# The first norm of a Hyena / mLSTM step, moved from token rows to feature rows

## The chip, the cores and the metric

The kernel runs on one core of one Trainium2 chip. The metric is the device time of one execution in microseconds, the median of three runs. Five engines matter. PE multiplies matrices (PEld is its weight load), DVE, ACT and POOL work element by element, and SP issues most of the DMA transfers. They meet only through semaphores.

## The reference

One layer of a diffusion backbone over 1024 latent tokens and 128 prompt tokens, each of 1024 features. What the change touches is the first norm and what it feeds:

```python
def _rmsnorm(x, w):
    xf = x.astype(F32)
    y = xf * lax.rsqrt(jnp.mean(xf * xf, axis=-1, keepdims=True) + EPS)
    return (y * w.astype(F32)).astype(x.dtype)
...
    h = _rmsnorm(x, p['norm_mix_w']) * (1 + scale_m) + shift_m
    proj = h @ p['w_in']
```

The mean of squares is over the features of one token; gain and shift differ for latent and prompt tokens. Beside it the reference makes the spectrum of a filter `k` from a small network, long before the projection needs it. Convolution, mLSTM, output projection, second norm and feed forward follow and are not touched.

## The kernel before, in words

Tokens come in nine tiles of 128, features in eight chunks of 128 (`KD`). Every large product is fp32 in three passes: each operand is split into a rounded part `hi` and a remainder `lo`, and `product` (lines 231, 233, 235) adds hi·hi, hi·lo and lo·hi in PSUM. A split costs one ACT instruction (hi) and one on DVE or POOL (lo).

**Stage A, the filter's spectra** (`filter_and_spectra`, one block of all engines). Twelve steps `spectrum(g)`, g = 0 to 11, of 24 matmuls of 256 columns each, write two PSUM banks each, in a ring of four pairs, `pair(g)`. For each step ACT copies one bank (L2072) and DVE combines it with the other (L2187 and L2188, or L2191); that signals `read`. After three steps a quarter of the spectrum is finished by `butterflies`, four instructions (L1628 to L1631): the first three quarters on POOL, the last one on DVE at the end of the block. SP stores each quarter to DRAM. Beside them the first norm runs by token row: x, nine tiles of 128 tokens by 1024 features, stays in SBUF; ACT takes the squares with their sum (L316), one tile in each step, DVE makes the means (L322), ACT the roots (L327), DVE the reciprocals (L332), ACT scales x in place (L337, nine instructions). SP loads x after the last modulation weights. POOL also splits two weight units (L180).

**Stage B, the projection** (`project_and_hyena`, the next block; a block starts when all engines have left the one before). x must stand by feature for the projection, so PE turns each chunk of it by transposes (`norm_chunk`, L1018): 24 chunks, eight for each group of tokens (`GROUPS`: tiles 0 to 2, 3 to 6, 7 and 8; in columns `PIECES`). DVE reads each turned chunk from PSUM with gain and shift (L1372), ACT makes hi (L1198), POOL two of three lo and DVE the third (L637). PE works on the projection's first two blocks of 128 outputs (items 0 and 1) piece by piece, as chunks come: piece 0 for both items (with the other 16 chunks' transposes between), piece 1, piece 2. From item 2 on PE works item by item.

Ahead of item 2 PE takes the first three parts of a last modulation product (`last_modulation`, L1054). Their weights, `rownorm_ada`, three megabytes, lie where the spectra of stage A lay, so SP loads them (L716) only after both stores of each spectrum buffer have landed (`spec_out`). Behind these loads in SP's queue stands the next weight unit (L892).

Of the kernel before, what the change touches and what calls it, by code (L numbers as in the profile page):

```python
# [23 lines left out]
P = 128  # L24
# [263 lines left out]
class RowNorm:  # L288
# [5 lines left out]
    def __init__(self, nc, io, ph):  # L294
        self.nc, self.io = nc, io
        self.x = ph.sb("x", [P, NT, D])
# [3 lines left out]
    def semaphores(self, ph):  # L300
        self.x_in = [ph.sem(f"x_in{t}") for t in range(NT)]
# [5 lines left out]
    def load(self, sp, g, tiles=None):  # L307
        for t in (range(3 * g, 3 * g + 3) if tiles is None else tiles):
            src = self.io["x_sample"][0, t * P:(t + 1) * P, :] if t < 8 else self.io["x_prompt"][0]
            sp.dma_start(self.x[:, t, :], src).then_inc(self.x_in[t], 16)  # L310

    def squares(self, act, t):
        act.wait_ge(self.x_in[t], 16)
        if t:
            act.wait_ge(self.summed, t)
        self.nc.scalar.activation(self.square[:], self.x[:, t, :], ACT.Square, accum_out=self.sum_sq[:, t:t + 1])\  # L316
            .then_inc(self.summed, 1)

    def mean(self, dve, g):
        s = slice(3 * g, 3 * g + 3)  # L320
        dve.wait_ge(self.summed, 3 * g + 3)
        self.nc.vector.tensor_scalar(self.mean_sq[:, s], self.sum_sq[:, s], 1.0 / D, EPS, ALU.mult, ALU.add).then_inc(self.means, 1)  # L322

    def take_root(self, act, g):
        s = slice(3 * g, 3 * g + 3)
# [3 lines left out]
    def invert(self, dve, g):  # L329
        s = slice(3 * g, 3 * g + 3)  # L330
# [14 lines left out]
PIECES = ((0, 384), (384, 896), (896, WT))  # L345

# [51 lines left out]
def project_and_hyena(nc, io, mem, dram, x, h_hi, h_lo, stage, first_memory, spec_out, last_out, ahead):  # L398
# [40 lines left out]
    full = [flat_stage[:, 512 * i:512 * i + 512] for i in range(4)] + [mem["gates"][:, 512 * i:512 * i + 512] for i in range(2)]  # L439
    with Phase(nc, "proj") as ph:  # L440
        ps, par = mem["psum"], mem["par"]
        flat = ps[:].rearrange("p b c -> p (b c)")
        turned = ph.sem("chunk_transposed")
        full_done = ph.sem("h_full_done")
# [175 lines left out]
        def lo_splitter(n):  # L620
            return "dve" if n % 3 == 2 else "pool"
# [7 lines left out]
        def chunk(n):  # L629
            g = n // KD  # L630
            a = full[n % FULL][:, 0:P * len(GROUPS[g])]
            return a.rearrange("p (t c) -> p t c", c=P) if g == 2 else a
# [78 lines left out]
        def _(sp):  # L711
# [6 lines left out]

            for i in range(2):
# [237 lines left out]
        def _(pool):  # L957
# [5 lines left out]
            for n in range(CHUNKS):  # L963
                if lo_splitter(n) == "pool":
                    split_chunk_lo(nc.gpsimd, n)
                if n == 18:
                    split_unit_lo(1)
# [44 lines left out]
        def _(pe):  # L1012
            def norm_chunk(n):
                g, k = n // KD, n % KD
                if n >= 2:
                    pe.wait_ge(full_done, n - 1)
                for i, t in enumerate(GROUPS[g]):
                    last = nc.tensor.transpose(ps[:, 6 + n % 2, i * P:(i + 1) * P], x[:, t, k * P:(k + 1) * P], mem["ident"][:])  # L1018
                last.then_inc(turned, 1)

# [11 lines left out]
            for n in range(KD):  # L1032
                norm_chunk(n)
            pe.wait_ge(zeros_set, 4)
            weights_ready(pe, 0)
            for i in range(3):
                for n in range(2):
                    for k in range(KD):
# [3 lines left out]
                        if i == 0:  # L1042
                            norm_chunk(KD + KD * n + k)
# [3 lines left out]
            def last_modulation(n):  # L1047

                for k in ada_parts.get(n, ()):
                    pe.wait_ge(ada_in[k % ADA_RING], 16 * (k // ADA_RING + 1))  # L1050
                    if k == 0:
                        pe.wait_ge(full_done, CHUNKS)
# [136 lines left out]
        def _(act):  # L1189
# [5 lines left out]
            for n in range(CHUNKS):  # L1195
                g, k = n // KD, n % KD
                act.wait_ge(full_done, n + 1)
                nc.scalar.activation(columns(h_hi[:, k, :], g), chunk(n), ACT.Copy).then_inc(hi_done, 1)  # L1198
                if n == 13:
                    split_unit_hi(1)  # L1200
            act.wait_ge(turned, CHUNKS)
# [153 lines left out]
        def _(dve):  # L1355
# [8 lines left out]
            for n in range(CHUNKS):  # L1364
                g, k = n // KD, n % KD
                dve.wait_ge(turned, n + 1)
                if n >= FULL:
                    wait_lo(dve, n - FULL)
                w = P * len(GROUPS[g])
                parts = ((0, w, 0),) if g < 2 else ((0, P, 0), (P, 2 * P, 1))  # L1370
                for a, z, j in parts:
                    ins = nc.vector.tensor_scalar(full[n % FULL][:, a:z], ps[:, 6 + n % 2, a:z], mem["gain_mix"][:, k, j:j + 1],  # L1372
                                                  mem["mod"][:, k, j:j + 1], ALU.mult, ALU.add)
                ins.then_inc(full_done, 1)
                if n >= 2 and lo_splitter(n - 2) == "dve":
                    split_chunk_lo(nc.vector, n - 2)
            split_chunk_lo(nc.vector, CHUNKS - 1)

            step = Chain(dve, step_sem)
# [268 lines left out]
def filter_and_spectra(nc, io, mem, dram, buffers, k_hi, k_lo, norm, stage, spec_out):  # L1648
# [7 lines left out]
    with Phase(nc, "kt") as ph:  # L1656
# [4 lines left out]
        spec = ph.sb("spec", [P, 2, 8, HC2])  # L1661
        flat_stage = stage[:].rearrange("p s t -> p (s t)")
        parts_of = [ph.sb("parts", [P, 8, HC2])[:], flat_stage[:, 0:8 * HC2].rearrange("p (a c) -> p a c", a=8)]
        third = ph.sb("third", [P, 2, HC2])
# [50 lines left out]
        last_spec = ph.sem("last_spectrum_done")  # L1715
# [4 lines left out]
        norm.semaphores(ph)  # L1720
# [1823 lines left out]
```

## Time and profile before

| | us |
|---|---|
| median of 3 runs | 1608.75 (1605.62 to 1608.81) |
| the profiled execution, its own time | 1604.54 |
| its span | 1602.7 |
| PE busy | 1537.1, 96% of the span |
| DVE, ACT, POOL busy | 989.1, 478.5, 468.4 |

The span is what the profiler saw from the first to the last instruction. Busy time counts no waits. PE is busy nearly everywhere, so what is left to win or lose is where it isn't. The lines "idle before" name who released an engine.

### The profile page before, as it was taken

What the parts mean: (1) busy time and instruction counts of PE and PEld (TensorE: products, weight loads), DVE (VectorE), ACT (ScalarE), POOL (GpSimd) and SP (SyncE); (2) the same over time, 40 slices, a digit from 0 to 9 for tenths busy, and PEclk for the clock granted to TensorE, in tenths of its full rate; (3) what the DMA queues carried; (4) which work ended last, traced back from release to release, by engine and by line L of the source; (5) the groups of instructions that cost most, each with busy time, mean ns of one, the idle gap of its engine ahead of it and who ended that gap; (6) DMA issues with size and microseconds to landing.
All of it is one profiled execution on the core that took longest, in us unless ns stands there. A gap on an engine that the chain in (4) does not pass through costs nothing.

```text
span 1602.7 us, 22372 instructions
## 1 busy us (share of the span) xinstructions
PE 1537.1 (96%) x9469; PEld 1419.5 (89%) x9469; DVE 989.1 (62%) x1370; ACT 478.5 (30%) x673; POOL 468.4 (29%) x209
## 2 busy tenths in 40 slices
PE   5889999999999988999999999999999999999997
PEld 2487899999999888998899999999999999999996
DVE  5757134788424447426788548846882886388846
ACT  2574122222433457225322112202220131022203
POOL 1665213211311167154232213312232222132210
PEclk9899999999999999999999999999999999999999
DMA  9753423443545786410101101011011110101102
GB/s 358 292 210 113 184 71 110 161 163 110 194 140 186 251 268 211 150 47 1 53 27 54 53 27 53 27 53 51 28 53 39 41 52 29 53 27 53 53 14 119
DMA packets 116039, 167.55 MB, mean 105 GB/s; under 512 B 6252, under 2 KB 95460, under 8 KB 110820
## 3 DMA queue, kind: packets, MB, share of 16 engines
q1 hardware_dynamic: 113887, 163.72, 29.7%
q10 hardware_dynamic: 2052, 2.40, 0.4%
q8 instruction: 75, 1.23, 0.3%
q14 instruction: 25, 0.20, 0.0%
HBM read 134.83 MB, written 31.27 MB: 104 GB/s over the span
## 4 chain that ended last, share of the span: by engine, by line
PE 58%; DVE 2%; ACT 0%; issue 0%; POOL 0%; ACTq 0%; DVEq 0%
PE psum L231 19%; PE psum L233 19%; PE psum L235 19%; DVE mlp_acc_a L3197 1%; PE psum L3447 0%; PE psum L3289 0%; DVE w_raw L3266 0%; DVE mlp_acc_a L3266 0%; DVE tail_x L3221 0%; DVE mlp_h_lo L3128 0%; PE psum L3328 0%; DVE w_raw L3118 0%; PE psum L3339 0%; DVE mlp_h_lo L3069 0%; ACT mlp_acc_a L3016 0%
## 5 line engine op out<-in xcount | busy, mean ns | idle before, releaser
L231 PE MATMUL psum<-mlp_h_hi,w_hi 128*128 128x384 f32 (+2 forms) x1248 | 307.1, 339 | 10.6 <-DVE mlp_h_lo L3069 6.6
L233 PE MATMUL psum<-mlp_h_lo,w_hi 128*128 128x384 f32 (+2 forms) x1248 | 303.9, 337 | 0.0
L235 PE MATMUL psum<-mlp_h_hi,w_lo 128*128 128x384 f32 (+2 forms) x1248 | 303.5, 336 | 0.0
L3197 DVE SCALAR_TENSOR_TENSOR w_raw<-psum,par,w_raw 128x945 f32<-128x945 f32 (+2 forms) x176 | 214.7, 1220 | 90.8 <-ACT w_raw L3016 87.1
L3197 DVE SCALAR_TENSOR_TENSOR mlp_acc_a<-psum,par,mlp_acc_a 128x945 f32<-128x945 f32 (+2 forms) x176 | 214.4, 1219 | 33.1 <-ACT mlp_acc_a L3016 29.9
L2800 POOL TENSOR_TENSOR w_lo<-w_raw,w_hi 128x2048 fp32r<-128x2048 f32 x32 | 148.1, 4629 | 288.4 <-ACT w_hi L2794 288.4
L231 PEld LDWEIGHTS psum<-mlp_h_hi,w_hi 128*128 128x128 f32 x1248 | 206.2, 189 | 29.1 <-DVE mlp_h_lo L3069 6.8
L233 PEld LDWEIGHTS psum<-mlp_h_lo,w_hi 128*128 128x128 f32 x1248 | 206.5, 189 | 15.4
L235 PEld LDWEIGHTS psum<-mlp_h_hi,w_lo 128*128 128x128 f32 x1248 | 206.0, 189 | 15.4
L3221 DVE SCALAR_TENSOR_TENSOR tail_x<-psum,mod,tail_x 128x384 f32<-128x384 f32 (+1 forms) x192 | 94.8, 515 | 128.4 <-PE psum L235 128.1
L233 PE MATMUL psum<-tail_g_lo,w_hi 128*128 128x384 f32 x480 | 160.5, 334 | 0.0
L231 PE MATMUL psum<-tail_g_hi,w_hi 128*128 128x384 f32 x480 | 160.5, 334 | 0.0
L235 PE MATMUL psum<-tail_g_hi,w_lo 128*128 128x384 f32 x480 | 160.5, 334 | 0.0
L231 PE MATMUL psum<-head_big_hi,w_hi 128*128 128x384 f32 (+3 forms) x578 | 146.7, 335 | 1.2 <-issue 1.2
L233 PE MATMUL psum<-head_big_lo,w_hi 128*128 128x384 f32 (+3 forms) x578 | 144.1, 330 | 0.0
L235 PE MATMUL psum<-head_big_hi,w_lo 128*128 128x384 f32 (+3 forms) x578 | 144.1, 330 | 0.0
L2900 POOL TENSOR_TENSOR tail_g_lo<-mlp_acc_a,tail_g_hi 128x1152 fp32r<-128x1152 f32 x20 | 53.8, 2691 | 249.3 <-ACT tail_g_hi L3029 249.3
L960 POOL TENSOR_TENSOR w_lo<-w_raw,w_hi 128x2048 fp32r<-128x2048 f32 (+1 forms) x13 | 60.3, 4639 | 195.6 <-ACT w_hi L1193 195.6
L231 PEld LDWEIGHTS psum<-head_big_hi,w_hi 128*128 128x128 f32 x578 | 98.0, 190 | 13.0 <-issue 6.5
L235 PEld LDWEIGHTS psum<-head_big_hi,w_lo 128*128 128x128 f32 x578 | 97.7, 190 | 7.2
L233 PEld LDWEIGHTS psum<-head_big_lo,w_hi 128*128 128x128 f32 x578 | 97.7, 190 | 7.0
L2794 ACT ACTIVATE w_hi<-w_raw 128x2048 fp32r<-128x2048 f32 x32 | 61.1, 1909 | 127.6 <-PE psum L235 127.6
(375 smaller groups left out, 2446.8 us busy)
## 6 DMA issues: line engine op xcount, KB each, us to landing
w_raw<-ffn_w_up SPq DMA_DIRECT2D x22, 1024.0 KB, 4.9
filt_ada<-ada_w SPq DMA_DIRECT2D x16, 1024.0 KB, 9.6
w_raw<-w_in SPq DMA_DIRECT2D x13, 1024.0 KB, 5.7
w_raw<-ffn_w_down SPq DMA_DIRECT2D x11, 1024.0 KB, 4.9
rownorm_ada<-ada_w SPq DMA_DIRECT2D x8, 1024.0 KB, 6.7
scan_spread<-scratch_scan_rows SPq DMA_DIRECT2D x16, 512.0 KB, 5.7
tail_x<-x_by_feature SPq DMA_DIRECT2D x8, 576.0 KB, 7.0
rownorm_x<-x_sample SPq DMA_DIRECT2D x8, 512.0 KB, 5.9
```

Of the source, the lines that this page charges most:

```text
L231: ins = nc.tensor.matmul(out, wh, x_hi(k, i), start=begin, stop=False)
L233: ins = nc.tensor.matmul(out, wh, x_lo(k, i), start=False, stop=False)
L235: ins = nc.tensor.matmul(out, wl, x_hi(k, i), start=False, stop=end)
L960: nc.gpsimd.tensor_tensor(weight_part("lo", u), raw(u), weight_part("hi", u).bitcast(F32), ALU.subtract)\
L2794: nc.scalar.activation(w_hi[:, u % 2, :], w_raw, ACT.Copy).then_inc(w_hi_done, 1)
L2800: nc.gpsimd.tensor_tensor(w_lo[:, u % 2, :], w_raw, w_hi[:, u % 2, :].bitcast(F32), ALU.subtract).then_inc(w_lo_done, 1)
L2900: nc.gpsimd.tensor_tensor(lo, acc_a[:, j, :], hi.bitcast(F32), ALU.subtract).then_inc(g_lo_done, 1)
L3197: ins = stt(out=out, in0=image(up_at)[:, r0 + dy:r1 + dy, c0 + dx:c1 + dx], scalar=weight(i, loc, t), in1=out, op0=ALU.mult, op1=ALU.add)
L3221: ins = stt(out=out, in0=src[:, a:z], scalar=gate[:, j:j + 1], in1=out, op0=ALU.mult, op1=ALU.add)
```

## The change

x is loaded by feature, in eight loads from an input that the kernel has already, and stays so. The squares still need token rows: nine tiles go through a ring of three buffers, each refilled only after the square three before it. SP issues these loads between the two weight units, so the stores of the spectra stand behind them. Squares come in other steps: two in steps 3, 4, 6 and 7, one in step 5. Means, roots and reciprocals go by the groups of 3, 4 and 2 tiles.

A token's factor now has to stand along a row of PSUM on every partition. ACT makes a diagonal of each tile's factors (nine instructions of 128x128), PE multiplies it by ones (`spread`), in bank 6 ahead of spectrum step 8, in bank 7 ahead of step 9, and the last two tiles in stage B. Banks 6 and 7 leave the ring of pairs after step 6. DVE scales chunks with `scale_x`: 13 of 24 in stage A beside steps 9 to 11, 11 in stage B. The shift is added by ACT with hi and by DVE with lo; chunks of the last group take two instructions each, since latent and prompt tokens differ. All lo are DVE's now. The transposes, L1372 and L337 are gone. The last quarter's butterflies move behind all of this on DVE in stage B, and SP waits for them ahead of its store and the loads of `rownorm_ada`. POOL splits weight unit 1 as its first work in stage B. The scratch memory for dynamic DMA is set to 1024 bytes.

```diff
+    def load_rows(self, sp, t):
+        if t >= TOKEN_ROWS:
+            sp.wait_ge(self.summed, t - TOKEN_ROWS + 1)
+        src = self.io["x_sample"][0, t * P:(t + 1) * P, :] if t < 8 else self.io["x_prompt"][0]
+        sp.dma_start(self.rows[:, t % TOKEN_ROWS, :], src).then_inc(self.rows_in[t % TOKEN_ROWS], 16)
...
-    def scale(self, act, g):
+    def diagonals(self, act, ident, g):
         act.wait_ge(self.rstds, g + 1)
-        for t in range(3 * g, 3 * g + 3):
-            self.nc.scalar.activation(self.x[:, t, :], self.x[:, t, :], ACT.Copy, scale=self.rstd[:, t:t + 1])
+        if g:
+            act.wait_ge(self.spread_done, g)
+        for i, t in enumerate(GROUPS[g]):
+            ins = self.nc.scalar.activation(self.diag[:, i, :], ident, ACT.Copy, scale=self.rstd[:, t:t + 1])
+        ins.then_inc(self.diag_done, 1)
+
+    def spread(self, pe, ones, out, g):
+        pe.wait_ge(self.diag_done, g + 1)
+        for i in range(len(GROUPS[g])):
+            ins = self.nc.tensor.matmul(out[:, i * P:(i + 1) * P], ones, self.diag[:, i, :], start=True, stop=True)
+        ins.then_inc(self.spread_done, 1)
+SCRATCH = 1024
+FIRST_SCALED = 13
+TOKEN_ROWS = 3
...
+def scale_x(nc, mem, x, n, done):
+
+    g, k = n // KD, n % KD
+    a0 = PIECES[g][0]
+    parts = ((a0, PIECES[g][1], 0),) if g < 2 else ((a0, LS, 0), (LS, T, 1))
+    for a, z, j in parts:
+        ins = nc.vector.scalar_tensor_tensor(out=x[:, k, a:z], in0=x[:, k, a:z], scalar=mem["gain_mix"][:, k, j:j + 1],
+                                             in1=mem["psum"][:, spread_bank(g), a - a0:z - a0], op0=ALU.mult, op1=ALU.mult)
+    ins.then_inc(done, 1)
...
         def split_chunk_lo(eng, n):
             g, k = n // KD, n % KD
             eng.wait_ge(hi_done, n + 1)
-            eng.tensor_tensor(columns(h_lo[:, k, :], g), chunk(n), columns(h_hi[:, k, :], g).bitcast(F32), ALU.subtract)\
-               .then_inc(lo_by[lo_splitter(n)], 1)
+            for out, src, hi, j in chunk_parts(n):
+                ins = nc.vector.scalar_tensor_tensor(out=columns(h_lo[:, k, :], g) if out is None else columns(h_lo[:, k, :], g)[:, out], in0=src,
+                                                     scalar=mem["mod"][:, k, j:j + 1], in1=hi.bitcast(F32), op0=ALU.add, op1=ALU.subtract)
+            ins.then_inc(lo_by["dve"], 1)
...
+            sp.wait_ge(last_spec, 1)
+            sp.dma_start(dram["kt"][3], first_memory["spec"]).then_inc(spec_out[1], 16)
             for i in range(2):
                 sp.wait_ge(spec_out[i], 32)
             for k in range(ADA_RING):
...
-            for n in range(KD):
-                norm_chunk(n)
             pe.wait_ge(zeros_set, 4)
             weights_ready(pe, 0)
             for i in range(3):
...
-                        if i == 0:
-                            norm_chunk(KD + KD * n + k)
+                    if (i, n) == (0, 0):
+                        pe.wait_ge(lo_by["dve"], KD)
+                        for j, t in enumerate(GROUPS[2]):
+                            spread = nc.tensor.matmul(ps[:, spread_bank(2), j * P:(j + 1) * P], mem["ones"][:], first_memory["diag"][:, j, :],
+                                                      start=True, stop=True)
+                        spread.then_inc(last_spread, 1)
...
+            step = Chain(dve, step_sem)
+            for n in range(KD):
+                split_chunk_lo(nc.vector, n)
+                if n >= KD - (2 * KD - FIRST_SCALED):
+                    scale_x(nc, mem, x, n + KD, full_done)
+            for n in range(KD, 2 * KD):
+                split_chunk_lo(nc.vector, n)
+            dve.wait_ge(last_spread, 1)
+            for n in range(2 * KD, CHUNKS):
+                scale_x(nc, mem, x, n, full_done)
+                if n > 2 * KD:
+                    split_chunk_lo(nc.vector, n - 1)
             split_chunk_lo(nc.vector, CHUNKS - 1)
-
-            step = Chain(dve, step_sem)
+            dve.wait_ge(spec_out[1], 16)
+            butterflies(step, tt, first_memory["spec"], first_memory["parts"])
+            dve.sem_inc(last_spec, 1)
...
+        SQUARES_AT = {3: (0, 1), 4: (2, 3), 5: (4,), 6: (5, 6), 7: (7, 8)}
+        MEANS_AT, ROOTS_AT, INVERTED_AT, SPREAD_AT = (5, 7, 8), (5, 7, 8), (6, 8, 9), (8, 9)
+        SCALED_AT = {8: range(0, 4), 9: range(4, 9), 10: range(9, FIRST_SCALED)}
...
-            first = (2, 0, 6, 4)[g % 4]
+            first = (2, 0, 6, 4, 2, 0, 6, 4, 2, 0, 4, 2)[g]
...
-            for u in range(2):
-                load_w_in(sp, ring, io, u, 3 + u)
+            load_w_in(sp, ring, io, 0, 3)
+            for t in range(NT):
+                norm.load_rows(sp, t)
+            load_w_in(sp, ring, io, 1, 4)
...
             for g in range(3, 12):
                 if g == 4:
                     pe.wait_ge(prompt_read, 1)
+                if g in SPREAD_AT:
+                    i = SPREAD_AT.index(g)
+                    if i == 0:
+                        pe.wait_ge(read, 7)
+                    norm.spread(pe, mem["ones"][:], ps[:, spread_bank(i), :], i)
                 spectrum(g)
```

## Rows read from the trace of the kernel before

**Rows 1.** The page, part 1: busy time, share and instructions of PE.

```profile
PE 1537.1 (96%) x9469; PEld 1419.5 (89%) x9469; DVE 989.1 (62%) x1370; ACT 478.5 (30%) x673; POOL 468.4 (29%) x209
```

**Rows 2.** Busy time in two stretches; the first line names the columns.

```profile
core 0: us, PE busy (x) PEld busy (x) DVE busy (x) ACT busy (x) POOL busy (x), PEclk, DMA share, GB/s
100.00:110.00 10.00, 10.00 (x87) 10.00 (x87) 4.12 (x8) 10.00 (x17) 9.59 (x6) 1.00 0.40 167
112.00:118.00 6.00, 0.51 (x3) 0.55 (x4) 4.63 (x13) 3.27 (x4) 1.73 (x2) 0.71 0.52 218
```

**Rows 3.** Timeline, PE: start us, us, instruction [idle before <-releaser].

```profile
111.14 0.28 PE L235 MATMUL psum<-head_big_hi,w_lo 128*128 128x256 f32 x1
117.49 4.51 PE L1018 MATMUL psum<-ident,rownorm_x 128*128 128x128 f32 x18 [6.07 <-PEq L259]
...
124.38 0.42 PE L231 MATMUL psum<-head_big_hi,w_hi 128*128 128x384 f32 x1
...
139.86 0.48 PE L231 MATMUL psum<-head_big_hi,w_hi 128*128 128x512 f32 x1
...
151.08 0.28 PE L231 MATMUL psum<-head_big_hi,w_hi 128*128 128x258 f32 x1
...
156.90 2.76 PE L1054 MATMUL psum<-rownorm_ada,par 128*2 128x512 f32 x24
159.59 0.68 PE L231 MATMUL psum<-head_big_hi,w_hi 128*128 128x384 f32 x2
```

**Rows 4.** Timeline, ACT, beside the filter's spectra.

```profile
89.41 1.05 ACT L316 ACTIVATE rownorm_square<-rownorm_x 128x1024 f32<-128x1024 f32 x1
...
93.32 1.28 ACT L327 ACT_TABLE_LOAD   x1
...
95.20 1.91 ACT L176 ACTIVATE w_hi<-w_raw 128x2048 fp32r<-128x2048 f32 x1
...
101.17 0.58 ACT L2072 ACTIVATE kt_parts<-psum 128x512 f32<-128x512 f32 x1
```

**Rows 5.** Timeline, DVE, same stretch.

```profile
89.54 0.69 DVE L2187 TENSOR_TENSOR head_stage<-psum,head_stage 128x512 f32<-128x512 f32 x1 [2.04 <-ACT head_stage L2072]
...
90.61 2.11 DVE L322 TENSOR_SCALAR rownorm_mean_sq<-rownorm_sum_sq 128x3 f32<-128x3 f32 x1
...
115.84 0.69 DVE L1631 TENSOR_TENSOR kt_spec<-head_stage 128x512 f32<-128x512 f32 x1
```

**Rows 6.** Timeline, POOL, same stretch.

```profile
88.07 4.63 POOL L180 TENSOR_TENSOR w_lo<-w_raw,w_hi 128x2048 fp32r<-128x2048 f32 x1 [12.72 <-ACT w_hi L176]
```

**Rows 7.** Timeline, SP queue: a line is the issue, not the transfer.

```profile
116.61 0.32 SPq L1826 DMA_DIRECT2D scratch_kt<-kt_spec  x1
120.47 1.28 SPq L716 DMA_DIRECT2D rownorm_ada<-ada_w  x3
```

**Rows 8.** Tile rownorm_ada, the three loads issued at 120 to 122 us.

```profile
DMA to landing us min/median/max: 4.8/6.9/8.8
```

**Rows 9.** DMA issues at 76 us: KB each, us to landing.

```profile
w_raw<-k_fwd SPq DMA_DIRECT2D x1, 1024.0 KB, 4.9
```

**Rows 10.** Timeline, DVE, in the second norm.

```profile
723.87 1.14 DVE L3118 SCALAR_TENSOR_TENSOR mlp_acc_a<-tail_x,gain_ffn,psum 128x384 f32<-128x384 f32 x2
...
731.06 1.50 DVE L3128 SCALAR_TENSOR_TENSOR mlp_h_lo<-w_raw,mod,mlp_h_hi 128x384 fp32r<-128x384 f32 x1
...
742.59 1.41 DVE L3118 SCALAR_TENSOR_TENSOR w_raw<-tail_x,gain_ffn,psum 128x512 f32<-128x512 f32 x2 [0.28 <-PE psum L3339]
...
747.30 0.75 DVE L3128 SCALAR_TENSOR_TENSOR mlp_h_lo<-w_raw,mod,mlp_h_hi 128x512 fp32r<-128x512 f32 x1
...
762.52 0.59 DVE L3118 SCALAR_TENSOR_TENSOR w_raw<-tail_x,gain_ffn,psum 128x128 f32<-128x128 f32 x2
```

**Rows 11.** Timeline, POOL, in the second norm.

```profile
730.84 1.30 POOL L2858 TENSOR_TENSOR tail_scan_h<-tail_scan_h 128x512 f32<-128x512 f32 x1 [1.96 <-ACT tail_scan_h L2945]
```

**Rows 12.** Timeline, PE, in the second norm.

```profile
741.49 1.06 PE L3339 MATMUL psum<-mlp_acc_a,ones 128*128 128x128 f32 x8
```

**Rows 13.** Timeline, ACT, in the second norm.

```profile
760.03 1.28 ACT L2955 ACTIVATE mlp_h_hi<-mlp_acc_a,mod 128x128 fp32r<-128x128 f32 x4 [0.84 <-DVE mlp_acc_a L3118]
```

More of the change, by code:

```diff
@@ L295, in __init__, with late @@
         self.nc, self.io = nc, io
-        self.x = ph.sb("x", [P, NT, D])
+        self.x = ph.sb("x", [P, KD, T])
         self.square = ph.sb("square", [P, D])
         self.sum_sq, self.mean_sq, self.root, self.rstd = (ph.sb(n, [P, NT]) for n in ("sum_sq", "mean_sq", "root", "rstd"))
-    def semaphores(self, ph):
-        self.x_in = [ph.sem(f"x_in{t}") for t in range(NT)]
+    def late(self, ph):
+        self.rows = ph.sb("token_rows", [P, TOKEN_ROWS, D])
+        self.diag = ph.sb("diagonals", [P, 4, P])
+        self.x_in = ph.sem("x_by_feature_in")
+        self.rows_in = [ph.sem(f"token_rows_in{i}") for i in range(TOKEN_ROWS)]
         self.summed = ph.sem("squares_summed")
@@ L305, in semaphores, with load, tiles @@
         self.rstds = ph.sem("rstds")
[L307 to L310, printed above, removed]
+        self.diag_done = ph.sem("diagonals_done")
+        self.spread_done = ph.sem("rstd_spread")
+        self.scaled = ph.sem("x_scaled")
+    def load_rows(self, sp, t):
[3 more added lines that the diff above has]
+        sp.dma_start(self.rows[:, t % TOKEN_ROWS, :], src).then_inc(self.rows_in[t % TOKEN_ROWS], 16)
+    def load(self, sp, k):
+        sp.dma_start(self.x[:, k, :], self.io["x_by_feature"][k]).then_inc(self.x_in, 16)
     def squares(self, act, t):
-        act.wait_ge(self.x_in[t], 16)
+        act.wait_ge(self.rows_in[t % TOKEN_ROWS], 16 * (t // TOKEN_ROWS + 1))
         if t:
             act.wait_ge(self.summed, t)
-        self.nc.scalar.activation(self.square[:], self.x[:, t, :], ACT.Square, accum_out=self.sum_sq[:, t:t + 1])\
+        self.nc.scalar.activation(self.square[:], self.rows[:, t % TOKEN_ROWS, :], ACT.Square, accum_out=self.sum_sq[:, t:t + 1])\
             .then_inc(self.summed, 1)
+    def tiles(self, g):
+        return slice(GROUPS[g][0], GROUPS[g][-1] + 1)
     def mean(self, dve, g):
-        s = slice(3 * g, 3 * g + 3)
-        dve.wait_ge(self.summed, 3 * g + 3)
+        s = self.tiles(g)
+        dve.wait_ge(self.summed, s.stop)
         self.nc.vector.tensor_scalar(self.mean_sq[:, s], self.sum_sq[:, s], 1.0 / D, EPS, ALU.mult, ALU.add).then_inc(self.means, 1)
     def take_root(self, act, g):
-        s = slice(3 * g, 3 * g + 3)
+        s = self.tiles(g)
         act.wait_ge(self.means, g + 1)
@@ L620, in lo_splitter @@
         def lo_splitter(n):
[L621 removed]
+            return "dve"
         def wait_lo(eng, n):
@@ L629, in chunk, with chunk_parts @@
         def chunk(n):
-            g = n // KD
-            a = full[n % FULL][:, 0:P * len(GROUPS[g])]
-            return a.rearrange("p (t c) -> p t c", c=P) if g == 2 else a
+            g, k = n // KD, n % KD
+            return x[:, k, 896:T].rearrange("p (t c) -> p t c", c=P) if g == 2 else x[:, k, PIECES[g][0]:PIECES[g][1]]
+        def chunk_parts(n):
+            g, k = n // KD, n % KD
+            hi = columns(h_hi[:, k, :], g)
+            if g < 2:
+                return [(None, chunk(n), hi, 0)]
+            return [(j, chunk(n)[:, j], hi[:, j], j) for j in range(2)]
         def split_chunk_lo(eng, n):
@@ L2066, in _ @@
                     copy_sums()
+                if g in INVERTED_AT:
+                    norm.diagonals(act, mem["ident"][:], INVERTED_AT.index(g))
                 act.wait_ge(full, sums_at(g))
@@ L2196, in _ @@
                     nc.vector.tensor_copy(prompt, pair(0)).then_inc(prompt_read, 1)
-            dve.wait_ge(read, 12)
-            dve.wait_ge(spec_out[1], 16)
-            butterflies(step, tt, spec[:, 1], parts_of[1])
-            dve.sem_inc(last_spec, 1)
+    return last_spectrum
 G_SRC, G_FLOOR, G_STATE = range(3)
```

89 lines of the change are left out of this document (39 added, 50 removed).

## The prediction

> **What bounds the kernel now.** I read the page first. PE is busy 96% of the span [rows 1], so a change far from PE's gaps is worth nothing, and whatever holds PE at the border of the two stages is paid in full: from item 2 on PE goes from product to product. The mark to follow is therefore the start of item 2's product, 159.59 us [rows 3]. Next I read the busy time by stretches and PE's timeline up to that mark. PE is full through the spectra [rows 2] until about 111.4, idle for 6.1 us, turns chunks from 117.49, begins products at 124.38 and finishes items 0 and 1 at 156.90 [rows 3]. In between, 512-column pieces take 11.2 us (139.86 to 151.08) and the last pieces 5.8; by columns the first would take 8.4, together 25.4 us of products in 39.4 us. About 14 us hang on the transposes and on the block's start. That is what the change goes for. Last I read the queue of SP: the last quarter's store at 116.61, the three loads for the modulation from 120.47 [rows 7]. The slowest lands 8.8 us after its issue [rows 8], at 130.2. PE takes them at 156.90: 27 us of cover now.
>
> **Stage A, where the change makes the steps late.** A step is 24 matmuls, 87 run in 10 us [rows 2], so 2.8 us; steps 8 to 11 begin at about 100.0, 102.8, 105.6 and 108.5.
>
> ACT's chain, from its first square after the copy of step 3 at 89.41 [rows 4]: a square costs 1.05 and its accumulator's read, 1.14 when two follow each other. Squares 0 and 1, the copy of step 4 (0.5) and square 2 end near 93.1. Square 3 needs the refill of the first buffer, issued when square 0 has ended, near 90.6. What does a lone half megabyte take? No row has one. A lone megabyte took 4.9 us [rows 9], and two of the three modulation loads followed the first in 5.0 us (landings 125.3 and 130.2, rows 8 and the issue times), so half a megabyte less is 1.2 us less: 3.7 us, with 2.5 and 5.0 as ends. It lands near 94.6. Then square 3, copy 5, the weight split (1.8), square 4, table load and root (1.5) [rows 4], a reciprocal, three diagonals at 0.31 [rows 13] and copy 6: 102.4. DVE's adds, 1.07 [rows 5], make it 103.5. Before, copy 6 was hardly earlier, 101.17 [rows 4], but nobody needed it. Now PE waits for this read ahead of the spread at step 8, from 100.0 on: **3.5 us**. Then squares 5 to 7 and copy 7; square 8 waits for its buffer, 107.7; root, reciprocal, four diagonals: 111.1. The second spread waits for that, another 4 us of PE. The means cost more than their work: one of 128x3 took 2.11 us [rows 5], until POOL's weight split of 4.63 ended [rows 6]. The second mean now falls into the other such split, whose end I put at 108.3; it is hidden behind square 8. The seven spreads are 0.25 each [rows 12], 1.8 us, inside these delays.
>
> From copy 8 (111.6) DVE ends the stage: 13 scalings, eight of 384 columns at 0.53 and five of 512 at 0.66 (pairs take 1.14 and 1.41, overlapping) [rows 10], 7.5 us; adds of steps 8 to 11, 3.4; about 1.2 of waits for step 9: **123.7**. With 0.9 for the change of blocks (116.53 to 117.49 now, rows 5 and 3) stage B starts at 124.6 and not 117.5. Ends: 122.5 if half megabytes land in 2.5 us, 126.8 if in 5. The four butterflies that leave (2.9 us) are subtracted, they don't show in this sum.
>
> The Trainium skill gives a price for the refill. The page "DMA: Bandwidth & Descriptors" (section "Anatomy of one DMA") has about 2.0 us fixed plus bytes over 436 GB/s, 3.2 us for a tile. By it stage B would start 0.5 us earlier. No row here shows a lone tile.
>
> **Stage B on PE.** A hi and a lo must exist first (1.2 us); then 25.4 us of products and two spreads, 0.4, and some 2 us for the first products at 1.2 GHz: items 0 and 1 end near 154. Alone, that is a gain of 3 us over 156.90 in spite of the late start.
>
> **Stage B on DVE, and what hangs on it.** DVE's order: 8 lo of 384 (0.53), 3 scalings of 512 (0.66), 8 lo of 512 (0.66; one took 0.75, rows 10), then for each of 8 chunks two scalings and two lo of 128 columns (pairs about 0.52 each): 4.2 + 2.0 + 5.3 + 8.3, plus 0.6 for the first hi and 0.2 at the last: 20.6. The lo read two tensors from SBUF. Such an instruction took 1.50 instead of 0.6 us when POOL's ran from 730.84 to 732.14 [rows 10, 11]. POOL splits weight unit 1 right in this stretch, 4.63 [rows 6], of which about 3.6 falls on DVE since a scaling from PSUM can pass. Then the butterflies, 4 x 0.72 [rows 5]: 2.9. Sum 27.1 from 124.6: the last quarter is ready at **151.7**, not 116.53, **35.1 us later**. Behind it everything in SP's queue moves alike: store, loads. The third load lands at 130.2 + 35.1 = 165.3. PE, done near 154, waits; only 27 us of cover were there. The last part takes 0.9 (2.76 for three, rows 3), so item 2's product starts at 166.2 and not 159.59, +6.6. The weight unit queued behind the loads is needed only at item 4, 25 us later; it costs nothing.
>
> The clock adds to it. Idle before 117.49 took the granted clock to 0.71 of full speed over 112 to 118 [rows 2], that is 1.2 GHz in part of it, and the 18 transposes after it took 4.51 us, with waits [rows 3]. PE now idles some 7 us again in front of item 2. If the last part and some 2 us of products run at half speed, that is 0.9 + 1.0; ends 0 and 3.5. I take 1.9.
>
> **Sum.** +6.6 + 1.9 = +8.5 us for the profiled execution, 1604.54 to 1613.0. The median shown lies 4.2 above that execution; on it, 1608.75 + 8.5 = **1617.3**.
>
> The setting of the DMA scratch memory and 4.7 MB more of loads (eight of 576 KB and nine of 512 against nine) are costed at nothing: stage A's refills are in the chain above, the first six feature loads are 0.4 MB longer, 1 us of transfers behind the decay loads, whose cover is one step of PE. Should that be gone: +1.
>
> **Rivals.** First, *the pair of ports doesn't stop DVE*: POOL's split is held back instead. For it: the lo come back to back. Against it: 731.06, where POOL had started. Then the last quarter is ready at 148.1, item 2 starts 3.6 earlier, +4.9: 1613.7. The page "SBUF — State Buffer" of the Trainium skill (section "SBUF: two separate sides") says that whoever starts first keeps the pair for the whole instruction; by that rule either order can come.
>
> Second, *the steps don't slip*: the last quarter must be ready by 143.2 for no loss at all (151.7 - 8.5), by 140.0 for a gain over 0.2%. That asks for stage B by about 116 and for POOL's split to cost nothing: 116 + 23.5 = 139.5, the third load at 153.2, item 2 at 156.0 with the last part and the clock, -3.6: 1605.1, **faster**. For it: PE alone would gain. Against it: ACT's copy of step 6 at 101.17 is late already and gets more in front of it.
>
> Third, *in between*: stage B at 119 or 120 and a cheaper clock, or refills in 2.5 us with the first rival: +0 to +3, about 1610.5, no change.
>
> Fourth, *slower still*: refills in 5 us and the full price of the clock, 2.2 + 1.6 more: 1621.1.
>
> **Chances.** Forecast with the first and fourth rival 0.75 (0.45, 0.15, 0.15), no change 0.17, faster 0.08. The measurement tells 0.2%, 3.2 us, from no change. The range 1608.0 to 1622.5 leaves out the faster case and the ends of both sides.
>
> **What the new profile would show.** PE idle ahead of spectrum steps 8 and 9, 3 to 4 us each, released by DVE's add of step 6 and ACT's diagonals; the last add of stage A near 123; first product near 126; one lo of 4 to 5 us while POOL splits; the butterflies near 150; the loads of rownorm_ada near 156; PE idle from about 154 to 163, its clock at half after it. If the idle time ahead of L1054 is missing, the central step is wrong. If the butterflies stand there by 141, stage A's or DVE's sum was too dark and the kernel is faster.

## The result, and the profile after

The changed kernel takes 1618.1 us (median of 4 runs, 1617.4 to 1619.3), the kernel before 1607.2 on the same chip (4 runs, 1603.7 to 1608.8): ratio 1.0068, 95% interval 1.0055 to 1.0081. It is slower by 10.9 us (the interval of the ratio makes it 8.8 to 13.0); the forecast of 1617.3 was 8.5 above its base. The profiled execution took 1619.34 us, its span 1617.5.

The page's row of PE, part 1 (busy, share, instructions), answers to [rows 1]; the two lines of stretches under it to [rows 2], with the same columns (PE, PEld, DVE, ACT, POOL busy, granted clock, DMA share, GB/s).

```profile
PE 1539.8 (95%) x9415; PEld 1419.1 (88%) x9415; DVE 996.1 (62%) x1394; ACT 474.7 (29%) x681; POOL 452.6 (28%) x193
```

```profile
100.00:110.00 10.00, 7.13 (x49) 6.92 (x48) 5.09 (x4) 8.47 (x17) 9.41 (x6) 0.83 0.59 184
112.00:118.00 6.00, 4.93 (x29) 4.93 (x30) 2.85 (x6) 2.29 (x8) 1.36 (x2) 0.72 1.01 420
```

PE has 54 instructions fewer and is busy 2.7 us longer, because part of its work runs at half clock. It was full from 100 to 110; now it is idle for 2.9 us there.

PE's timeline of the changed kernel (start, duration, instruction, idle time before and its releaser) answers to [rows 3]. The first two lines are the spreads of the norm ahead of spectrum steps 8 and 9, the third is the product of stage B that waited for the first lo, the L1100 lines are the three parts of the modulation, the last is item 2's first product.

```profile
105.12 0.93 PE L358 MATMUL psum<-kt_diagonals,ones 128*128 128x128 f32 x6 [2.87 <-DVE kt_parts L2255]
113.07 1.77 PE L358 MATMUL psum<-kt_diagonals,ones 128*128 128x128 f32 x8 [2.66 <-ACT kt_diagonals L352]
129.21 0.66 PE L231 MATMUL psum<-head_big_hi,w_hi 128*128 128x384 f32 x1 [4.93 <-DVE head_big_lo L686]
...
163.88 1.89 PE L1100 MATMUL psum<-rownorm_ada,par 128*2 128x512 f32 x8 [6.58 <-DMA rownorm_ada<-ada_w]
166.51 1.89 PE L1100 MATMUL psum<-rownorm_ada,par 128*2 128x512 f32 x8 [0.75 <-DMA rownorm_ada<-ada_w]
168.94 1.89 PE L1100 MATMUL psum<-rownorm_ada,par 128*2 128x512 f32 x8 [0.55 <-DMA rownorm_ada<-ada_w]
170.76 1.33 PE L231 MATMUL psum<-head_big_hi,w_hi 128*128 128x384 f32 x3
```

Before, the 24 modulation matmuls ran in one go, 2.76 us with no wait, and item 2 followed at 159.59 [rows 3]. Now PE waits 7.9 us for loads (6.58, 0.75 and 0.55), and the same 24 take 5.7 us of matmul time (three lines of 1.89), twice as long: the granted clock over 165 to 170 us is 0.50.

DVE and POOL, timelines; they answer to [rows 5, 6]. L335 is the second mean, L2258 the last add of stage A, L1407 the first instruction of stage B, L686 the lo of the input and L1679 the last butterfly of the last quarter.

```profile
106.20 4.31 DVE L335 TENSOR_SCALAR rownorm_mean_sq<-rownorm_sum_sq 128x4 f32<-128x4 f32 x1 [1.13 <-ACT rownorm_square L326]
...
119.29 0.69 DVE L2254 TENSOR_TENSOR head_stage<-psum,head_stage 128x512 f32<-128x512 f32 x1 [2.91 <-ACT head_stage L2133]
...
126.81 0.69 DVE L2258 TENSOR_TENSOR head_stage<-psum,kt_third 128x512 f32<-128x512 f32 x1
127.86 0.06 DVE L1407 MEMSET psum<- 128x1 f32 x1 [0.36 <-PEq L259]
...
141.33 3.63 DVE L686 SCALAR_TENSOR_TENSOR head_big_lo<-rownorm_x,mod,head_big_hi 128x128 fp32r<-128x128 f32 x2 [0.25 <-ACT head_big_hi L1246]
...
154.15 0.69 DVE L1679 TENSOR_TENSOR kt_spec<-head_stage 128x512 f32<-128x512 f32 x1
```

```profile
105.89 4.58 POOL L180 TENSOR_TENSOR w_lo<-w_raw,w_hi 128x2048 fp32r<-128x2048 f32 x1 [0.18 <-POOL kt_spec L1679]
...
137.52 7.02 POOL L1013 TENSOR_TENSOR w_lo<-w_raw,w_hi 128x2048 fp32r<-128x2048 f32 x1 [15.56 <-ACT w_hi L1239]
```

The queue of SP, answering to [rows 7]: the last quarter's store, then the three loads; and the landing of these three, answering to [rows 8].

```profile
154.93 0.32 SPq L771 DMA_DIRECT2D scratch_kt<-kt_spec  x1
158.78 1.57 SPq L767 DMA_DIRECT2D rownorm_ada<-ada_w  x3
```

```profile
DMA to landing us min/median/max: 5.1/7.3/8.9
```

The store moved from 116.61 to 154.93, the loads from 120.47 to 158.78: both by 38.3 us. The slowest of the three takes 8.9 us to land, as before (8.8).

**How the two traces are set against each other.** The whole execution was late before any line of the change ran: the load of k_fwd [rows 9] was issued at 75.93 us before and 78.08 after. In the profiles of all kernels of this study this mark lies between 75.93 and 78.11, in kernels without the change too (76.58, 77.19, 77.72). It is taken off. Two more marks then split each trace: the first memset of stage B (117.52 before), and the first store of scratch_hv (208.39 before, 90.87 after the memset), behind which SP's stores and weight loads follow each other in every kernel at the same distances, to 0.04 us, up to 417 us on the clock of before. All in us, ratios with their 95% intervals:

| kernel | k_fwd load | stage B start against before, k_fwd taken off | stage B to hv store, against before | sum | median against before, same chip | ratio |
|---|---|---|---|---|---|---|
| changed | 78.08 | +8.2 | 93.56, +2.7 | +10.9 | +10.9 | 1.0068 [1.0055, 1.0081] |
| e10, changed again | 77.50 | +8.1 | 93.79, +2.9 | +11.0 | +9.3 | 1.0056 [1.0044, 1.0068] |
| e1, loads apart | 77.04 | +6.6 | 80.54, -10.3 | -3.8 | -0.3 | 1.0000 [0.9988, 1.0011] |
| e9, e1 again | 77.76 | +8.2 | 80.96, -9.9 | -1.7 | -1.5 | 0.9986 [0.9976, 0.9995] |
| e2, POOL's split late | 76.06 | +8.2 | 88.69, -2.2 | +6.0 | +5.8 | 1.0043 [1.0028, 1.0057] |
| e3, quarter first | 78.11 | +8.8 | 84.01, -6.9 | +1.9 | +2.3 | 1.0012 [0.9999, 1.0025] |
| e4, later steps | 76.73 | +3.0 | 92.85, +2.0 | +5.0 | +7.2 | 1.0044 [1.0031, 1.0057] |
| e6, e1 and e4 | 77.17 | +3.6 | 81.32, -9.6 | -6.0 | -6.8 | 0.9963 [0.9952, 0.9974] |
| e5, before, scratch 1024 | 76.58 | 0.0 | 90.89, 0.0 | 0.0 | -0.3 | 1.0000 [0.9990, 1.0011] |
| e8, before, loads at 145 | 77.19 | -0.1 | 90.87, 0.0 | -0.1 | -1.7 | 0.9992 [0.9980, 1.0005] |
| e7, before, loads at 155 | 77.72 | 0.0 | 99.55, +8.7 | +8.7 | +7.7 | 1.0050 [1.0032, 1.0068] |

So the change costs 8.2 us up to the start of stage B and 2.7 behind it. The 2.7 is two large terms, a loss of 13.0 (93.56 against e1's 80.54) and a gain of 10.3. The table stops at the store of scratch_hv; what lies behind it, and how far it can be told, stands at the end of the experiments.

### The profile page after: what moved, and what is told of

The parts are those of the page before. It is cut to its first block, busy times and chain, and to the rows that moved or that the text cites. A ratio compares the mean times of both kernels' runs of the same rounds, so it can differ in the third digit from the quotient of the medians.

```text
span 1617.5 us, 22273 instructions
## 1 busy us (share of the span) xinstructions
PE 1539.8 (95%) x9415; PEld 1419.1 (88%) x9415; DVE 996.1 (62%) x1394; ACT 474.7 (29%) x681; POOL 452.6 (28%) x193
## 4 chain that ended last, share of the span: by engine, by line
PE 57%; DVE 2%; ACT 1%; issue 0%; POOL 0%; ACTq 0%; DVEq 0%
PE psum L231 19%; PE psum L235 19%; PE psum L233 19%; DVE mlp_acc_a L3261 1%; PE psum L3511 0%; DVE w_raw L3330 0%; DVE mlp_h_lo L3133 0%; DVE tail_scan_h L3139 0%; PE psum L3353 0%; DVE mlp_acc_a L3330 0%; DVE tail_x L3285 0%; DVE mlp_h_lo L3192 0%; PE psum L3392 0%; PE psum L3403 0%; DVE w_raw L3182 0%
```

## The experiments

Two theories were set against each other. By the first, the loss behind stage B's start is the chain of the prediction: last quarter, store, loads of the modulation in SP's order. By the second, DVE's or PE's own work in stage B is slower than thought, and the order in SP's queue is an onlooker.

**e1: the loads apart.** Their memory no longer overlaps the last quarter's, so they don't follow its store. The diff shows SP's order; the lines that place the three token rows between the two spectrum buffers are left out.

```diff
-            sp.wait_ge(last_spec, 1)
-            sp.dma_start(dram["kt"][3], first_memory["spec"]).then_inc(spec_out[1], 16)
             for i in range(2):
-                sp.wait_ge(spec_out[i], 32)
+                sp.wait_ge(spec_out[i], 32 - 16 * i)
             for k in range(ADA_RING):
                 load_ada(k)
+            sp.wait_ge(last_spec, 1)
+            sp.dma_start(dram["kt"][3], first_memory["spec"]).then_inc(spec_out[1], 16)
```

> The changed kernel, but the last quarter's spectrum no longer lies under the ring of modulation weights, so their three loads start with stage B and only the store waits for the last quarter. Theory (the loads behind the last quarter set the start of item 2): PE goes from items 0 and 1, which ended at 157.3, straight through the three parts (2.8 us) to item 2, near 160 and not 170.8, and the clock doesn't fall: 2.2 us more. Together 12.9 us less than the changed kernel's 1618.1, so 1605, ratio to before 0.999. Rival (stage A's later end costs it all): stage B starts at the same 127.8, so nothing or at most the 2 us of the clock come back, 1616.

Measured: 1605.25, ratio 1.0000, against 1.0068. SP's queue and PE's timeline of e1:

```profile
125.20 1.29 SPq L766 DMA_DIRECT2D rownorm_ada<-ada_w  x3
...
152.26 0.33 SPq L774 DMA_DIRECT2D scratch_kt<-kt_spec  x1
```

```profile
154.25 2.76 PE L1099 MATMUL psum<-rownorm_ada,par 128*2 128x512 f32 x24
```

The last quarter is ready as late as ever, 27.0 us after stage B's start (152.17 against 125.20; in the changed kernel 154.84 against 127.86, again 27.0), and nobody waits for it. PE goes into the modulation without a wait and needs 2.76 us for it, as before. The chain is the loss: 13.0 us. In the changed kernel's trace it is 7.9 of waits, 2.9 by which the 24 matmuls are longer, and 2.2 of item 2's first products at half clock.

**e7 and e8: the suspected cost alone, in the kernel before.** One wait of SP ahead of the three loads, nothing else.

```diff
             for i in range(2):
                 sp.wait_ge(spec_out[i], 32)
+            sp.wait_ge(center_done, 1)
             for k in range(ADA_RING):
                 load_ada(k)
```

> The suspected cost alone, in the kernel before: its three modulation loads wait until ACT has evacuated item 0, 155.5 us in its trace, where the prediction put them for the changed kernel. Nothing else is changed. Theory: the third lands 8.8 us after, 164.4; PE idles from 156.9 on and starts item 2 near 165.3 with the last part, 5.7 us late, and the granted clock falls there as in the changed kernel, 3.1 us more: +8.8, 1614.4, ratio 1.0055. Rival, the clock takes no more than 1 us after an idle stretch in which a few matmuls run: +6.7 or less, 1612.3. Rival, the loss of the changed kernel comes from elsewhere and the loads can be late: 1605.6 to 1608.

In e8 the wait is for `hi_done, CHUNKS` instead, ACT's last split of the input; in e7 it is for ACT's evacuation of item 0.

> As the last, but the loads wait only for ACT's last split of the normalised input, 144.7 us, 24 us later than in the kernel before. Theory: the cover of 27 us holds: the third lands near 153.6, ahead of 156.9, and nothing is lost: 1605.6, ratio 1.000 (0.999 to 1.001). Rival: three loads this late collide with other transfers or land later than 12 us, +1 to +3: 1607 to 1608.6.

Measured: e7 1614.3, ratio 1.0050; e8 1604.9, ratio 0.9992. PE's timeline of e7:

```profile
162.50 1.89 PE L1055 MATMUL psum<-rownorm_ada,par 128*2 128x512 f32 x8 [3.80 <-DMA rownorm_ada<-ada_w]
164.92 1.89 PE L1055 MATMUL psum<-rownorm_ada,par 128*2 128x512 f32 x8 [0.53 <-DMA rownorm_ada<-ada_w]
167.38 1.89 PE L1055 MATMUL psum<-rownorm_ada,par 128*2 128x512 f32 x8 [0.57 <-DMA rownorm_ada<-ada_w]
169.20 1.33 PE L231 MATMUL psum<-head_big_hi,w_hi 128*128 128x384 f32 x3
```

24 us of delay are free, 35 cost 8.7 between the two marks: 4.9 of waiting, and the 3.8 that are left are work at half clock, 2.9 in the three parts and 0.9 behind them (lines of 1.89; the granted clock is 0.50 over 165 to 170). The wait and the clock price of the changed kernel exist without any of the change. e8's loads are issued at 146.0 to 146.9 and land within 9.1 us, 2 us before PE takes them at 158.10. The rivals of a cheap clock (6.7 us or less) and of a cause elsewhere (3 us or less) fall by the 8.7 between the marks; the medians alone, 7.7 with an interval of 5.1 to 10.9, would leave the first open.

**e2: POOL's split after the quarter.**

```diff
                     split_chunk_lo(nc.gpsimd, n)
+            pool.wait_ge(last_spec, 1)
             split_unit_lo(1)
```

> The changed kernel, but POOL's split of weight unit 1 waits until DVE has finished the last quarter. Theory (DVE is stopped by POOL's port, and every us of DVE is a us of item 2's start): the 3.6 us that one lo waited are gone, the last quarter is ready at 151.2 and not 154.8, item 2 starts 3.6 us earlier, 1614.5. Rival (DVE has slack, the loads would be late anyway by the transfers alone): no change, 1618. Should POOL's split then hold item 2 itself, it would show as a wait for w_lo before item 2; it should end near 158, before the loads land.

Measured: 1611.4, ratio 1.0043, 4.0 us better than the changed kernel by the ratios and 4.9 by the marks. The last quarter is ready 24.0 us after stage B's start (149.80 against 125.82), not 27.0: POOL's share of DVE's time is 3.0 us. POOL's timeline of e2, and of e3 below, which has the butterflies ahead:

```profile
149.94 4.62 POOL L1013 TENSOR_TENSOR w_lo<-w_raw,w_hi 128x2048 fp32r<-128x2048 f32 x1 [30.35 <-DVEq L1428]
```

```profile
138.16 9.53 POOL L1013 TENSOR_TENSOR w_lo<-w_raw,w_hi 128x2048 fp32r<-128x2048 f32 x1 [16.44 <-ACT w_hi L1239]
```

Alone the split takes 4.62 us, beside DVE's row of lo 7.02 or 9.53. In e2 PE idles 3.4, 1.3 and 0.6 us ahead of the three parts instead of 6.6, 0.75 and 0.55.

**e3: the quarter first.** The four butterflies, 2.9 us, go to the head of DVE's order.

```diff
             step = Chain(dve, step_sem)
+            dve.wait_ge(spec_out[1], 16)
+            butterflies(step, tt, first_memory["spec"], first_memory["parts"])
+            dve.sem_inc(last_spec, 1)
             for n in range(KD):
                 split_chunk_lo(nc.vector, n)
```

> The changed kernel, but the last quarter's four instructions are the first work of DVE in stage B, ahead of the lo and the scalings. Theory: the last quarter is ready near 131, the loads land near 145, PE starts its products 2.9 us later and is then the bound: item 2 at 163.0 without the loss by the clock, 9.9 us less than the changed kernel, 1608.2. Rival (stage B's DVE chain is the bound, not the loads): 2.9 us more, 1621.

Measured: 1607.85, ratio 1.0012. The trace is that of the slowest of its ten executions (1613.3), so only its distances between marks are used. The loads are issued at 135.91 and covered. From stage B's start to the store it takes 3.5 us more than e1 (84.01 against 80.54), because the butterflies now stand in front of the first lo, for which PE waits: it begins 3.2 us after the stage's start and not 0.6.

**e4: later steps.** The two spreads stand ahead of steps 9 and 11 instead of 8 and 9, the mean of the second group behind the add of step 7 instead of ahead of it, the third group's mean, root and diagonals one step later. Six of the thirteen scalings come ahead of DVE's adds of steps 7 and 8.

```diff
-        MEANS_AT, ROOTS_AT, INVERTED_AT, SPREAD_AT = (5, 7, 8), (5, 7, 8), (6, 8, 9), (8, 9)
-        SCALED_AT = {8: range(0, 4), 9: range(4, 9), 10: range(9, FIRST_SCALED)}
+        MEANS_AT, ROOTS_AT, INVERTED_AT, SPREAD_AT = (5, 8, 9), (5, 7, 9), (6, 8, 10), (9, 11)
+        SCALED_AT = {6: range(0, 2), 7: range(2, 6), 8: range(6, 8), 9: range(8, 10), 10: range(10, FIRST_SCALED)}
```

> The changed kernel with the same instructions in other spectrum steps: spreads ahead of steps 9 and 11 instead of 8 and 9, the second mean behind the add of step 7 instead of ahead of it, the third group one step later, six of the thirteen scalings in steps 7 and 8. Theory (PE's two waits in stage A and the clock that falls with them make stage B late, DVE's scalings end it): PE doesn't wait ahead of step 8, stage B starts near 121.3 and not 127.8, and all of it goes into item 2's start since DVE's chain moves as a whole: 6.5 us less, 1611.6. Rival (DVE's sum of scalings and adds sets stage A's end whatever PE does): stage B at 126 to 128, 1617.

Measured: 1612.7, ratio 1.0044: 3.9 us better and not 6.5. Stage B started at 121.33 as expected, but the execution was an early one (k_fwd at 76.73). Against the changed kernel's 127.86, which was a late one, that looked like 6.5; with the starts taken off it is 8.2 - 3.0 = 5.2. The expectation had used a mark of two executions without setting them equal. What is left: PE's waits in stage A are 0.76 and 0.30 us instead of 2.87 and 2.66. Stage B is 0.7 shorter on top of it, which makes 5.9; the medians show 3.7 to 3.9, with an interval of 2 us on either side of each ratio. Where the other 2 us are is not shown.

**e6: e1 and e4 together.**

> The changed kernel with two edits at once: the modulation's loads ahead of the last quarter, in memory of their own (alone 1605.25), and the root, the diagonals and the last spread at later steps (alone 3.9 us better than the changed kernel). Theory: they add up, because the one takes the wait ahead of item 2 away and the other starts stage B earlier: stage B starts near 121, its loads are issued there, item 2 starts some 4 us earlier than with the loads alone, near 153.5, and the time is 1605.25 - 3.9 = 1601.3, ratio 0.9974, faster than before. Rival: stage B's PE work is then bound by something else, DVE's splits, or the gain is given back near 500 to 530 us where PE waits for hyi_y_lo; then 1603.5 to 1605.5, ratio about 0.9995.

Measured: 1599.9 (10 runs, 1598.9 to 1603.5), ratio 0.9963 [0.9952, 0.9974]: faster than the kernel before by 6.8 us and than the changed one by 1.0%. Its rival, 1603.5 to 1605.5, falls. One stretch of e6 (columns as in [rows 2]) shows stage A with no drop of the clock:

```profile
100.00:115.00 15.00, 14.01 (x115) 13.44 (x114) 10.58 (x21) 10.34 (x23) 9.21 (x5) 1.00 0.75 258
```

DVE's timeline of e6 at the border:

```profile
119.31 0.68 DVE L2258 TENSOR_TENSOR head_stage<-psum,kt_third 128x512 f32<-128x512 f32 x1
122.36 0.06 DVE L1406 MEMSET psum<- 128x1 f32 x1 [2.37 <-PEq L259]
```

DVE is done at 119.99 and the next stage starts 2.4 us later. SP issues the store of POOL's third quarter at 121.45 in this trace, so POOL's butterflies are probably the next bound. That was not tried.

**e5: before with the scratch setting.**

> The kernel before with only the changed kernel's setting of the DMA scratch memory, 1024 bytes. Theory: the setting costs nothing: 1605.6 us, ratio 1.000 (0.999 to 1.001). Rival: part of the loss is its doing, by slower DMA work; then 1608 or more. Its profile is read at two more places. Where the k_fwd load of unit 2 is issued: 75.93 us in the profile of before, 76.1 to 78.1 in the profiles of the changed kernel and of the four experiments so far; if executions differ there by themselves, it can stand anywhere in 75.9 to 78.1 here. And ahead of the product with hyi_i_hi near 523 us, where PE waits 0.6 to 2.0 us for hyi_y_lo in all kernels with the change and not at all in the profile of before: a wait of that size here belongs to the setting or to the execution; none speaks for the change itself.

Measured: 1606.3 beside 1606.6, ratio 1.0000. The setting costs nothing that can be measured. There is no wait for hyi_y_lo near 523 us either.

**e9 and e10: e1 and the changed kernel again.**

> The kernel of the experiment with the loads apart once more, for one thing left open. From the start of stage B to the first store of hv it took 80.54 us and the kernel before 90.87; with its later start that store comes some 3.8 us earlier than in the kernel before once the start of both executions is set equal. Yet the medians were equal: some 3 us are given back later. In its trace the lead shrinks by 2.1 us between 418 and 568 us, where PE waited 0.8 us for hyi_y_lo, and by 1.6 later. If this belongs to the kernel, this run shows it again: the lead of 2.6 to 3.8 at the store of hv, a wait for hyi_y_lo, the lead gone by 568 us, ratio 0.999 to 1.001. If it was that execution, the lead stays and the ratio is nearer to 0.998 (1603).

> The changed kernel once more beside it. Its first profile began 2.05 us late against that of before in work the change doesn't touch, and lost 2.2 more between 418 and 568 us. Expected: ratio 1.0068 as before; from stage B's start to the store of hv 93.6 us, as in the first profile, since that is the kernel's; the start another one of 0 to 2 us; and between 418 and 568 us again 2 us if that belongs to the changed order of the work, or 0 to 3 in no relation to it if it doesn't.

Measured: e9 1605.4, ratio 0.9986; e10 1616.2, ratio 1.0056. Neither reading of e1 came out whole. The distance from stage B to the store is the kernel's: 80.54 and 80.96, 93.56 and 93.79. But e1's stage B had started 1.6 us early, by luck. The stretches of e1, then of e9, show where:

```profile
102.00:107.00 5.00, 3.03 (x14) 3.03 (x15) 3.07 (x3) 4.44 (x9) 4.68 (x3) 0.62 0.43 155
107.00:112.00 5.00, 3.49 (x18) 3.28 (x17) 3.61 (x5) 2.68 (x8) 2.42 (x1) 0.70 0.97 296
112.00:117.00 5.00, 4.99 (x43) 5.00 (x44) 3.20 (x7) 1.83 (x5) 1.62 (x2) 1.00 0.96 401
```

```profile
102.00:107.00 5.00, 2.29 (x19) 2.29 (x20) 2.33 (x3) 4.90 (x10) 4.67 (x4) 1.00 0.50 174
107.00:112.00 5.00, 1.48 (x13) 1.27 (x11) 4.40 (x5) 2.16 (x7) 3.20 (x1) 1.00 0.97 275
112.00:117.00 5.00, 4.20 (x22) 4.20 (x23) 2.85 (x6) 2.02 (x7) 1.11 (x1) 0.66 1.03 431
```

In e1 the clock fell after the first idle time and was back before step 9, where time counts; in e9 (and e10) it stayed full over step 8, whose work hid in the second wait, and fell for step 9. The second wait is 4.3 us in e9 and e10, 1.5 in e1. What reaches stage B is DVE's wait for step 9: 1.33 us in e1 and 2.91 in e9, 1.6 apart.

```profile
116.65 0.69 DVE L2254 TENSOR_TENSOR head_stage<-psum,head_stage 128x512 f32<-128x512 f32 x1 [1.33 <-ACT head_stage L2133]
119.01 0.69 DVE L2254 TENSOR_TENSOR head_stage<-psum,head_stage 128x512 f32<-128x512 f32 x1 [2.91 <-ACT head_stage L2133]
```

What stays open: between 418 and 568 us on the clock of before the kernels with the change lose 2.2 (changed), 2.1 (e1), 1.5 (e2), 3.2 (e3), 2.1 (e4), 1.4 (e9) and 0.7 (e10) against the profile of before, with a wait of 0.6 to 2.0 us for hyi_y_lo in it; e6 loses 0.4, without that wait, and the three variants of before -0.5 (e5), 0.35 (e8) and 0.25 (e7). PE's arrival and the loads of that stretch seem to meet less well. Its cause was not tested. Behind 568 us it goes on to vary. From the first store of scratch_hv to the store of y_prompt it takes 1390.8 us before, 1392.5 and 1390.5 in the two executions of the changed kernel, 1394.4 in e1 and 1391.8 in e9, and 1389.8 in e6. So this stretch differs by 2.0 and 2.7 us between two executions of one kernel, and how much of it belongs to the change can't be told from these traces. In e1's own trace it takes back the whole lead of 3.8.

## Why the prediction was right

**The result.** +8.5 was forecast, +10.9 came; 1617.3 against 1618.1, the smaller miss because the median of before, with a fourth execution in it, came out 1.6 under the base. That part of the agreement is luck. The sum was 2.4 too small, in the two places below. The medians alone can't say so to a tenth: 8.5 lies just under the interval of 8.8 to 13.0 here and inside that of e10, 7.1 to 10.9. The marks of the two traces, 10.9 and 11.0, say it, but they end at the store of scratch_hv; that the median difference is 10.9 too is partly chance, given the 2 us by which the rest varies.

**Stage A: right in both waits, short by 1.2 us.** The waits stand where they were forecast, ahead of steps 8 and 9, released by DVE's add and ACT's diagonals: 2.87 and 2.66 us against 3.5 and 4 (2.7 and 4.3 in e10). DVE's add of step 6 ended at 105.06, less 2.15 is 102.9; forecast 103.5. The diagonals ended at 113.0, less 2.15 is 110.9; forecast 111.1. Refills: ACT's fourth square started at 96.19 after 0.75 us of waiting for its tile, which is 94.0 on the clock of before; forecast 94.6. The refills took 3.3 to 4.5 us to land, inside the ends 2.5 and 5.0; the one in the chain, issued at 92.64, took 3.5, and 3.7 was taken for it.

```profile
96.19 1.06 ACT L326 ACTIVATE rownorm_square<-kt_token_rows 128x1024 f32<-128x1024 f32 x1 [0.75 <-DMA kt_token_rows<-x_sample]
...
108.25 1.06 ACT L326 ACTIVATE rownorm_square<-kt_token_rows 128x1024 f32<-128x1024 f32 x1 [0.57 <-DMA kt_token_rows<-x_prompt]
```

The Trainium skill, in the page "DMA: Bandwidth & Descriptors", section "Anatomy of one DMA", gives its figure for transfers that GpSimd issues, and these loads go out on SP's queue. An estimate by that figure, 3.2 us, is 0.3 under the refill in the chain and 0.1 under the shortest one, so it was no nearer than the 3.7 where it counted.

The first of the two mis-sized terms is "about 1.2 of waits for step 9". DVE waited 2.91 us (the line at 119.29), 1.7 more, because PE began step 9 at half clock after its idle time: the granted clock is 0.72 over 112 to 118, and step 9's first matmuls take 0.41 us each (0.28 before [rows 3]). In e1, where step 9 ran at full clock, DVE waited 1.33, close to the forecast; in e9 and e10 2.91 and 2.89.

```profile
114.85 0.41 PE L233 MATMUL psum<-head_big_lo,w_hi 128*128 128x256 f32 x1
```

The last add ended at 127.50, less 2.15 is 125.35, against 123.7. The prediction charged the clock at item 2 and forgot it here, behind the very waits that it had forecast. At stage B's start 1.1 of this is left, 125.7 against 124.6, because the change of blocks took 0.4 us and not 0.9.

The mean beside POOL's split took 4.31 us for four columns and ended with it (110.51 and 110.47). It was forecast as hidden behind square 8. Square 8 ended at 109.4, the mean 1.1 later, and the root waited for it: not quite hidden.

**Stage B on PE: right.** Items 0 and 1 ended at 157.3, 29.4 us after the start; forecast 154 after 124.6, also 29.4. The gain of 10 us that was hoped for from the missing transposes is real: with the loads free, stage B up to the store is 10.3 us shorter than before in e1, 9.9 in e9 and 9.6 in e6.

**Stage B on DVE, and the chain: right to half a microsecond, in part by luck.** After stage B's start, forecast and measured: last quarter 27.1 and 27.0; issue of the loads 31.0 and 30.9; third load landed 40.7 and 41.1. The first rival, that POOL gives way, is half true: the price to DVE was 3.0 us (3.63 for a pair that takes 0.61) and not 3.6, and POOL lost 2.4 of its own (7.02 instead of 4.62). "One lo of 4 to 5 us" was really one of 3.4. DVE's own work made up for it: without POOL its last lo ends 21.2 us after stage B's start in e2 (147.0 against 125.82), and 20.6 was forecast. The two errors of 0.6 cancel in the 27.1. The rule of the page "SBUF — State Buffer", section "SBUF: two separate sides", of the Trainium skill, that the first to start keeps the pair for the whole instruction, fits the pair of lo that began at 141.33 and was done at 144.96, behind the end of POOL's split at 144.54. That POOL stays off while one lo of DVE follows another, 2.4 us here, is what the trace adds.

**The clock at item 2: mis-sized.** The prediction took 1.9 with ends 0 and 3.5. Measured: the last part took 1.89 instead of about 0.9, and after item 2's product had begun PE stayed at half clock for 4.4 us, some 2.2 of loss: 3.1. Counted the same way e7, which has only the late loads, loses the 1.9 that was taken: 1.0 in the last part and 0.9 behind item 2's start, where the clock is full again after some 2 us. So the price differs between runs whose waits look alike, and why is not shown. Stretches of the changed kernel:

```profile
160.00:165.00 5.00, 1.12 (x8) 0.11 (x8) 1.52 (x2) 0.00 (x0) 0.00 (x0) 0.62 0.91 362
165.00:170.00 5.00, 3.70 (x20) 0.22 (x16) 0.00 (x0) 0.00 (x0) 0.00 (x0) 0.50 1.02 403
170.00:175.00 5.00, 5.00 (x17) 3.85 (x14) 0.00 (x0) 1.91 (x1) 1.50 (x1) 0.51 1.04 425
```

The sum by the marks: 1.1 from stage A (8.2 against 7.1) and 1.3 from stage B (2.7 against 1.4), 2.4 in all, which is 10.9 - 8.5. The 1.3 is the clock, 3.1 against 1.9, with the third load landing 0.4 later than forecast (41.1 against 40.7); the terms add up to 1.6, 0.3 more than the marks allow.

**What was costed at nothing** stayed there for the scratch setting (e5) and the weight unit queued behind the loads (PE has no wait between item 2's start and the store of scratch_hv). For the longer loads ahead this is not shown as well: the k_fwd mark overlaps between both kinds of kernels, with 76.9 on average in the four without the change and 77.3 in the eight with it. The rival with the steps on time is what e4 made true by hand, and e6 shows that with the loads free it is indeed faster than before.

## What to carry to other kernels

When an edit delays a piece of work that looks idle, follow the queue behind its store: here a quarter of a spectrum that nobody needed for long held three loads that PE needed, and the cover of 27 us was spent to the last. In this kernel a delay inside the cover cost nothing (24 us, e8), and one beyond it cost its wait plus the clock (35 us: 4.9 + 3.8, e7), so count a price for work at half clock behind every forecast wait of PE, not only behind the last. And before two traces are compared, take off a mark from work that the edit doesn't touch; the 2 us by which these executions differed at the start are as large as most steps of such a sum.

## What the runs showed of the hardware

- A POOL instruction with its operands in SBUF that starts into a row of DVE's lo is held off while they run back to back: 4.62 us alone, 7.02 and 9.53 beside them (e2, changed, e3). It goes on when DVE turns to scalings with an operand in PSUM: 4.62 us before its end is 139.92 in the changed kernel and 143.07 in e3, and these scalings begin at 139.96 and 143.12. DVE's next lo then loses 3.0 us.
- An instruction of four columns on DVE took 4.31 us beside such a POOL instruction, and one of two columns 0.16 us behind it (changed).
- The same program meets the fall of the clock at different steps from one execution to the next: granted clock 0.62 in step 8 and 1.00 in step 9 (e1), 1.00 and 0.66 (e9). DVE's wait for step 9 and the start of stage B moved with it by 1.6 us.
